# Two layers and two blocks on one core: the inverse root of the row norms partly on GpSimd, the end of the kernel regrouped, retention's gates computed before its projections

## The reference

```python
# stage 0: h = rms_norm(x); stick-breaking attention and a state-space mixer; x = x + mix @ even_w_out
# stage 1: h = rms_norm(x); gated linear attention;                            x = x + mix @ odd_w_out
# stages 2 and 3 (one block each, l = 0 and 1 in the code):
#   h = rmsnorm(x) with scale and shift from c;  proj = h @ w_in
#   attention in three dilated groups, and retention
#   m = sigmoid(g_attn) * (att @ w_proj_attn) + sigmoid(g_ret) * (ret @ w_proj_ret)
#   x = x + gate * (m @ w_out)
# end: out = rmsnorm(x, final_norm_w)
def rms_norm(x, g):
    y = x * rsqrt(mean(x * x, axis=-1) + 1e-6)
    return y * g
```

## Time and profile before

| what | value |
|---|---|
| median of 3 runs | 1077.22 us (1075.8 to 1077.54) |
| the profiled execution | 1076.03 us |
| its span in the profile | 1074.2 us |
| PE busy | 1021.6 us, 95% of the span |
| DVE / ACT / POOL busy | 704.9 / 565.3 / 336.5 us |
| mean granted TensorE clock | 0.987 of full |

### The profile page before, as it was taken

One profiled execution on the slowest core, in us unless ns is written; L12 is line 12 of the kernel. 1 busy time (PEld: TensorE's weight loads), 2 busy tenths in 40 slices (PEclk: granted clock), 3 DMA queues, 4 the chain that ended last, 5 costly groups with the idle time before them and its releaser, 6 DMA issues.

```text
span 1074.2 us, 15495 instructions
## 1 busy us (share of the span) xinstructions
PE 1021.6 (95%) x6084; PEld 900.2 (84%) x6084; DVE 704.9 (66%) x1072; ACT 565.3 (53%) x872; POOL 336.5 (31%) x349
## 2 busy tenths in 40 slices
PE   5999999989999799999999989979999999999995
PEld 5778889878968689998899868868999888998884
DVE  7894856888767664455576686774544565667665
ACT  5978577557344754455443344455444555334552
POOL 4700150433530173552453545321744000320001
PEclk9999999999999999999999989999999999999998
DMA  8543424767736487765565556745877436644531
GB/s 277 154 141 101 141 93 140 251 206 246 216 113 215 145 266 217 241 200 153 177 214 178 164 170 206 225 128 177 249 216 216 122 118 177 185 148 147 187 137 59
DMA packets 94440, 191.12 MB, mean 178 GB/s; under 512 B 6768, under 2 KB 10096, under 8 KB 94368
## 3 DMA queue, kind: packets, MB, share of 16 engines
q1 hardware_dynamic: 86256, 164.71, 49.6%
q0 software_dynamic: 6960, 22.71, 6.8%
q10 hardware_dynamic: 1152, 2.72, 0.7%
HBM read 189.07 MB, written 1.05 MB: 177 GB/s over the span
## 4 chain that ended last, share of the span: by engine, by line
PE 86%; DVE 6%; ACT 5%; DMA 1%; issue 1%; DVEq 0%; SPq 0%; ACTq 0%
PE G L593 15%; PE G L595 14%; PE G L594 14%; PE G L602 8%; PE G L604 8%; PE G L605 8%; PE B L556 2%; DVE WL L1526 1%; ACT AR L1046 1%; ACT WH L1046 1%; PE G L631 1%; PE G L633 1%; PE G L632 1%; DMA RAW<-in_even_w_in 1%; PE B L905 1%
## 5 line engine op out<-in xcount | busy, mean ns | idle before, releaser
L1526 DVE TENSOR_TENSOR WL<-RAW,WH 128x1024 fp32r<-128x1024 f32 (+2 forms) x306 | 398.5, 1306 | 258.2 <-ACT WH L1046 257.4
L1046 ACT ACTIVATE WH<-RAW 128x1024 fp32r<-128x1024 f32 (+2 forms) x306 | 320.2, 1050 | 282.9 <-PE G L595 142.7
L593 PE MATMUL G<-WH,HTh 128*128 128x512 f32 (+1 forms) x564 | 227.7, 404 | 2.8 <-DVE WL L1526 2.5
L602 PE MATMUL G<-HTh,WH 128*128 128x256 f32 x768 | 220.2, 287 | 0.5 <-DVE HTl L1602 0.5
L595 PE MATMUL G<-WL,HTh 128*128 128x512 f32 (+1 forms) x564 | 218.7, 388 | 0.0
L604 PE MATMUL G<-HTl,WH 128*128 128x256 f32 x768 | 217.9, 284 | 0.0
L605 PE MATMUL G<-HTh,WL 128*128 128x256 f32 x768 | 217.8, 284 | 0.0
L594 PE MATMUL G<-WH,HTl 128*128 128x512 f32 (+1 forms) x564 | 217.8, 386 | 0.0
L602 PEld LDWEIGHTS G<-HTh,WH 128*128 128x128 f32 x768 | 147.1, 191 | 2.4 <-issue 2.2
L604 PEld LDWEIGHTS G<-HTl,WH 128*128 128x128 f32 x768 | 147.1, 191 | 0.9 <-issue 0.7
L605 PEld LDWEIGHTS G<-HTh,WL 128*128 128x128 f32 x768 | 147.0, 191 | 0.0
(11 more groups left out here) (344 smaller groups left out, 1343.9 us busy)
## 6 DMA issues: line engine op xcount, KB each, us to landing
RAW<-in_w_in SPq DMA_DIRECT2D x176, 512.0 KB, 3.8
RAW<-in_even_w_in SPq DMA_DIRECT2D x40, 512.0 KB, 3.7
AR<-in_w_ada POOLq DMA_DIRECT2D x80, 256.0 KB, 3.9
RAW<-in_odd_w_in SPq DMA_DIRECT2D x16, 512.0 KB, 4.9
RAW<-in_w_proj_ret SPq DMA_DIRECT2D x16, 512.0 KB, 3.5
RAW<-in_w_out SPq DMA_DIRECT2D x16, 512.0 KB, 4.2
RAW<-in_even_w_out SPq DMA_DIRECT2D x12, 512.0 KB, 3.9
AR<-in_w_ada SPq DMA_DIRECT2D x16, 256.0 KB, 4.3
```

Of the source, the lines that this page charges most:

```text
L593: nc.tensor.matmul(o, xh, wh, start=begins, stop=False)
L602: nc.tensor.matmul(o, fh, h_[:, kx, :], start=begins and f % 2 == 0, stop=False, skip_group_check=True)
L1046: return nc.scalar.activation(out_, ps, ACT.Copy, **kw)
L1526: vt(wl, raw, wh.bitcast(F32), ALU.subtract).then_inc(*dve.mark(LO, n))
```

## The change

- `rstd` is split. POOL's new `root(l, ti)` adds 1024 times epsilon to the sum of the first half, then the sum of the second (`MEAN`), and raises the result to the power -0.5 (`ROOT`). DVE's `rstd` makes -16 times the sum and takes one Newton step on POOL's value, three instructions in place of eleven (ten in norm 0).
- POOL calls `root` before each `scaled`; in stages 3 and norm 4 the root of tile 0 stands ahead of the half-0 add of tile 1 (`RES_P`).
- The end: SP loads `FW` in the middle of block 3's stream. The last residual add is cut in two, and ACT squares the two parts as they come. DVE multiplies (0,0) and (0,1) ahead of the last root, and (1,1) behind it; POOL makes `XW`, the product of (1,0) with `FW`, ahead of its last root, and ACT scales it. SP issues three stores and ACT one.
- In both blocks the groups run `gr0`, `gr1`, `pr0`, `pr1`; `gr1`'s tanh has a tile of its own (`T12b`, the space of `SZA2`), and the first two `mrg_turn`s move from steps 186 and 187 to 194 and 195.

```diff
-AT_MRG = (186, 187, 202, 203)
+AT_MRG = (194, 195, 202, 203)
...
+        NSE = [cols(2) for _ in range(5)]
+        neg_half = cols(1)
...
             for i in range(2):
                 group(("gr", l, i), "N", WI, 10240 + 512 * i, 512, K8, ht, banks())
+            for i in range(2):
                 group(("pr", l, i), "N", t["w_proj_ret_2"][l], 512 * i, 512, K8, lambda k: (YTh, YTl, 4 + k), banks())
...
-                            act.wait_ge(*MRG.of(l, 0, ti))
-                        nc.scalar.activation(T12[:, ti, :], ps[:, :], ACT.Tanh, scale=0.5).then_inc(
+                            act.wait_ge(*ATT_G.of(l))
+                        nc.scalar.activation((T12b if (kind, i) == ("gr", 1) else T12)[:, ti, :], ps[:, :], ACT.Tanh, scale=0.5).then_inc(
                             *act.mark(SIG, kind, l, i, ti))
...
-            for ti in range(2):
-                for n in range(2):
-                    square(3, ti, n)
-            nc.scalar.dma_start(FW, t["final_norm_w_2"].rearrange("(a n) -> a n", a=1).partition_broadcast(P)).then_inc(
-                l_fw, 16)
-            xs = X[:, 0, 512:1024]
-            act.wait_ge(*RSTD.of(4, 0))
-            copy(xs, xs, scale=NR[4][:, 0:1]).then_inc(*act.mark(FIN_A, "x"))
-            act.wait_ge(*FIN_P.of(0, 1))
-            nc.scalar.dma_start(out[0, 0:128, 512:1024], xs).then_inc(s_out[1], 16)
-            act.wait_ge(*FIN.of(1, 1))
-            nc.scalar.dma_start(out[0, 128:256, 512:1024], X[:, 1, 512:1024]).then_inc(s_out[3], 16)
+            square(3, 0, 0)
+            square(3, 0, 1)
+            square(3, 1, 0)
+            for j in range(2):
+                c = slice(512 + 256 * j, 768 + 256 * j)
+                act.wait_ge(*FIN_X.of(j))
+                nc.scalar.activation(TK[:, 1, 1, 256 * j:256 * j + 256], X[:, 1, c], ACT.Square,
+                                     accum_out=ss_last if j else NSS[4][:, 3:4]).then_inc(
+                    *(act.mark(FIN_SQ, "last") if j else act.mark(SUMSQ, 4, 1, 1)))
+            act.wait_ge(*RSTD.of(4, 1))
+            act.wait_ge(*FIN_W.of("x"))
+            copy(X[:, 1, 0:512], XW, scale=NR[4][:, 1:2]).then_inc(*act.mark(FIN_A, "x"))
+            act.wait_ge(*FIN_A.of("x"))
+            nc.scalar.dma_start(out[0, 128:256, 0:512], X[:, 1, 0:512]).then_inc(s_out[2], 16)
...
-                i, h, z, e, v = (x[:, k] for x in (rs_i, rs_h, rs_z, rs_e, rs_v))
-                inv = 1.0 / 1024
-                if l == 0:
-                    dve.wait_ge(*SUMSQ.of(0, ti))
-                    ts(v, NSS[0][:, k], inv, EPS, ALU.mult, ALU.add).then_inc(*dve.tick())
-                else:
-                    dve.wait_ge(*SUMSQ.of(l, ti, 0))
-                    ts(e, NSS[l][:, k], inv, EPS, ALU.mult, ALU.add).then_inc(*dve.tick())
-                    dve.wait_ge(*dve.prev)
-                    dve.wait_ge(*SUMSQ.of(l, ti, 1))
-                    ts(v, NSS[l][:, 2 + ti:3 + ti], inv, e, ALU.mult, ALU.add).then_inc(*dve.tick())
+                h, z = (x[:, k] for x in (rs_h, rs_z))
+                dve.wait_ge(*MEAN.of(l, ti))
+                ts(h, NSE[l][:, k], -16.0, None, ALU.mult).then_inc(*dve.tick())
                 dve.wait_ge(*dve.prev)
-                ts(i.bitcast(I32), v.bitcast(I32), 1, None, ALU.logical_shift_right).then_inc(*dve.tick())
-                first = dve.prev
-                ts(h, v, -0.5, 0.0, ALU.mult, ALU.add).then_inc(*dve.tick())
-                half = dve.prev
-                dve.wait_ge(*first)
-                ts(y.bitcast(I32), i.bitcast(I32), -1.0, MAGIC, ALU.mult, ALU.add).then_inc(*dve.tick())
-                dve.wait_ge(*half)
-                for step in range(3):
-                    dve.wait_ge(*dve.prev)
-                    stt(z, y, h, y, ALU.mult, ALU.mult).then_inc(*dve.tick())
-                    dve.wait_ge(*dve.prev)
-                    stt(y, z, 1.5, y, ALU.add, ALU.mult).then_inc(*(dve.tick() if step < 2 else dve.mark(RSTD, l, ti)))
+                dve.wait_ge(*ROOT.of(l, ti))
+                stt(z, y, h, y, ALU.mult, ALU.mult).then_inc(*dve.tick())
+                dve.wait_ge(*dve.prev)
+                stt(y, z, 48.0, y, ALU.add, ALU.mult).then_inc(*dve.mark(RSTD, l, ti))
...
-                        stt(T12[:, ti, :], T12[:, ti, :], 1.0, ps[:, :], ALU.add, ALU.mult).then_inc(*dve.tick())
+                        s = (T12, T12b)[i][:, ti, :]
+                        stt(s, s, 1.0, ps[:, :], ALU.add, ALU.mult).then_inc(*dve.tick())
                         dve.wait_ge(*dve.prev)
                         dve.wait_ge(*MRG_A.of(l, i, ti))
-                        vt(m, m, T12[:, ti, :], ALU.add).then_inc(*dve.mark(MRG, l, i, ti))
+                        vt(m, m, s, ALU.add).then_inc(*dve.mark(MRG, l, i, ti))
...
+                    if (l, ti) == (1, 1):
+                        for j in range(2):
+                            c = slice(256 * j, 256 * j + 256)
+                            vt(x[:, c], x[:, c], G2[:, 1, c], ALU.add).then_inc(*dve.mark(FIN_X, j))
+                        return
...
-            rstd(4, 1)
-            for ti, n in ((0, 0), (1, 0), (1, 1)):
+            dve.wait_ge(l_fw, 16)
+            for ti, n in ((0, 0), (0, 1), (1, 1)):
                 c = slice(512 * n, 512 * n + 512)
                 xs = X[:, ti, c]
+                if ti:
+                    rstd(4, 1)
                 dve.wait_ge(*RSTD.of(4, ti))
-                dve.wait_ge(l_fw, 16)
-                stt(xs, xs, NR[4][:, ti:ti + 1], FW[:, c], ALU.mult, ALU.mult).then_inc(*dve.mark(FIN, ti, n))
+                stt(xs, xs, NR[4][:, ti:ti + 1], FW[:, c], ALU.mult, ALU.mult).then_inc(*dve.mark(FIN_V, ti, n))
...
+            def root(l, ti):
+                e, y = NSE[l][:, ti:ti + 1], NR[l][:, ti:ti + 1]
+                pool.wait_ge(*SUMSQ.of(l, ti, 0) if l else SUMSQ.of(0, ti))
+                gts(e, NSS[l][:, ti:ti + 1], 1024 * EPS, 0.0, ALU.add, ALU.add).then_inc(
+                    *(pool.tick() if l else pool.mark(MEAN, 0, ti)))
+                own()
+                if l:
+                    pool.wait_ge(*SUMSQ.of(l, ti, 1))
+                    gts(e, NSS[l][:, 2 + ti:3 + ti], e, 0.0, ALU.add, ALU.add).then_inc(
+                        *(pool.tick() if (l, ti) == (4, 1) else pool.mark(MEAN, l, ti)))
+                    own()
+                if (l, ti) == (4, 1):
+                    pool.wait_ge(*FIN_SQ.of("last"))
+                    gts(e, ss_last, e, 0.0, ALU.add, ALU.add).then_inc(*pool.mark(MEAN, l, ti))
+                    own()
+                gtt(y, e, neg_half, ALU.pow).then_inc(*pool.mark(ROOT, l, ti))
...
+            nc.gpsimd.memset(neg_half, -0.5).then_inc(*pool.tick())
             for ti in range(2):
+                root(0, ti)
                 scaled(0, ti)
...
             for ti in range(2):
+                root(1, ti)
                 scaled(1, ti)
...
+                    if ti == 0:
+                        root(2 + l, 0)
+                scaled(2 + l, 0)
+                root(2 + l, 1)
+                scaled(2 + l, 1)
                 for step in range(212):
                     time = 2 * H0[l] + step
...
+                if ti == 0:
+                    root(4, 0)
             pool.wait_ge(l_fw, 16)
-            gtt(x, x, FW[:, 512:1024], ALU.mult).then_inc(*pool.mark(FIN_P, 0, 1))
+            own()
+            gtt(XW, x, FW[:, 0:512], ALU.mult).then_inc(*pool.mark(FIN_W, "x"))
+            root(4, 1)
...
+                if n == H0[1] + 54:
+                    sp.wait_ge(*ADA_P.of(1, 63))
+                    nc.sync.dma_start(FW, t["final_norm_w_2"].rearrange("(a n) -> a n", a=1).partition_broadcast(
+                        P)).then_inc(l_fw, 16)
+            for ti, n in ((0, 0), (0, 1), (1, 1)):
+                sp.wait_ge(*FIN_V.of(ti, n))
+                nc.sync.dma_start(out[0, 128 * ti:128 * ti + 128, 512 * n:512 * n + 512],
+                                  X[:, ti, 512 * n:512 * n + 512]).then_inc(s_out[2 * ti + n], 16)
             for s in s_out:
                 sp.wait_ge(s, 16)
```

More of the change, by code:

```diff
@@ L288, in program @@
         FW = AR[:, 1024:2048]
+        XW = flat(QKT[:, 0:2, :])
+        ss_last = cols(1)
         WE, WEO, WG = t["even_w_in"][0], t["even_w_out"][0], t["s5_w_glu"][0]
@@ L427, in program @@
         SUMSQ = events("sumsq", [(0, 0), (0, 1)] + [(l, ti, n) for l in range(1, 5) for ti in L2 for n in L2])
+        MEAN, ROOT = (events(f"norm_{x}", [(l, ti) for l in range(5) for ti in L2]) for x in ("mean", "root"))
         RSTD = events("rstd", [(l, ti) for l in range(5) for ti in L2])
```

12 lines of the change are left out of this document (3 added, 9 removed).

## The result

The changed kernel takes 1068.79 us, the median of six runs. One of them took 1276.3 us at a mean clock of 0.752 and is left out of the ratio; the other five lie between 1065.52 and 1071.91, and their median is 1068.22. The kernel before, measured beside it, takes 1076.68. The ratio is 0.992 with a 95% interval of 0.9896 to 0.9945, so the gain is about 8 us where 11.6 were forecast. The time lies inside the range and 3.2 us above the predicted 1065.6. Measured again in a later group of runs it came to 1067.65 (ratio 0.9909, 0.9897 to 0.9922).

A forecast was written before the change was run, and what follows sets the result against it. Bound by what keeps TensorE (95% busy) waiting or lies before its first and after its last product. Start +0.7, boundaries -1.9, -2.4, -1.5, clock -2.2, end -4.3, regrouping 0: -11.6 us, median 1065.6, range 1062.0 to 1071.5.

The forecast's parts named there:

- the start: Before TensorE's first product: roots queue behind POOL's memsets, moving that product from 16.40 to 17.1, a cost of 0.7 us.
- the end: After TensorE's last product: early FW load, products ahead of the root and an earlier last store gain 4.3 us.
- What the move is worth between the stages: Boundaries 0/1, 1/2 and 2/3: shorter DVE roots gain 1.9, 2.4 and 1.5 us, the second tile giving the larger gain.
- The power: POOL's power in each root: taken as 0.3 us, with a range of 0.15 to 1.3.
- Boundary 2/3: Between stages 2 and 3: POOL's order eats the first tile's gain, the second tile's mostly stays; 1.5 us gained.
- the moved add is hidden: At the end, POOL's tile 1 add moves 0.6 us behind tile 0's root, its square still done in time.
- The clock: Slow stretches at boundaries 1/2 and 2/3: 1.6 and 2.7 us at full clock; half taken, 2.2 us, bounds 0 and 4.3.
- rival 2: Boundaries 1/2 and 2/3: the clock falls as before, 2.2 us less gain, 1067.8 us; chance 0.14.
- rival 1: Boundaries 1/2 and 2/3: the clock stays up at both, 2.1 us more gain, 1063.5 us; chance 0.17.
- The regrouping: Gate groups in both blocks: the back-to-back merges fit, worth 0, with -0.3 to +1.0 us for both blocks.
- The slope of the power: Each us of power costs 2 at the start, 1 at boundary 2/3, 1 at the end; above 1.0 us, 2 more.
- the balance at 2.3 us: POOL's power length at which gain and loss are equal; beyond it the change is slower, chance 0.07 with rounding.

The follow-up runs named there:

- e11: Changed kernel with norm 0's roots and all roots of tile 0 back on DVE, POOL keeping four roots of tile 1: 1066.75 us, ratio 0.9909.
- e2: Changed kernel with all ten roots back on DVE in their old form, the new end and regrouping kept: 1075.66 us, ratio 0.9986.
- e3: Changed kernel with the two roots of norm 0 back on DVE: 1064.54 us, ratio 0.9875.
- e10: e9 with POOL's add of tile 1 also waiting for tile 0's finished root between stages 2 and 3: 1065.66 us, ratio 0.991.
- e12: The changed kernel once more, unaltered, in a later group of runs: 1067.65 us, ratio 0.9909.
- e8: e3 with the last residual add and its square uncut, so POOL's last root has two sums: 1064.22 us, ratio 0.9885.
- e9: e8 with POOL's add of tile 1 at the end waiting until DVE has finished tile 0's root: 1064.94 us, ratio 0.9889.
- e1: Kernel before with only the regrouped gates, including the second tanh tile and two moved turns: 1077.12 us, ratio 0.9998.
- e6: e3 with each of the eight remaining powers on POOL made twice in a row: 1068.18 us, ratio 0.9923.
- e4: Changed kernel with the roots of norm 0 and norm 4 back on DVE, POOL keeping the six at the boundaries: 1066.44 us, ratio 0.9889.
- e5: e3 with POOL's add of tile 1 again ahead of tile 0's root, at boundary 2/3 and the end: 1066.78 us, ratio 0.9911.
- e7: e3 with unread products filling TensorE's waits at the three boundaries: 1065.83 us, ratio 0.9904.

## Why the prediction was right, and where it was wrong

The sign, the order of size and the main mechanism held. The time came out 3.2 us above the forecast, because two terms of the sum, the start and the end, were too good by 1.0 and 2.75 us, and the clock's 0.8 us behind 1/2 did not come in this run. Behind 2/3 the forecast had 1.5 us and 1.35 for the clock; 3.4 came.

- **What the move is worth between the stages: right.** Second tiles: DVE is freed of 1.6 us (2.22 to 0.63 in the rows of boundary 1/2), POOL has the value long before, and tile 1 carries most of the gain (e11). From the first product to the turn at 2/3, 4.3 us were forecast without the clock, and 4.0 came. In e2, where DVE keeps the roots, the turning of tile 1 is back in its old place.
- **The power: mis-sized.** I took 0.3 us, near the row of a 128x16 product, with 0.15 to 1.3 as bounds. It is 0.56 or 0.57 in all ten of its instances. The bounds held it.
- **The start: mis-sized, +0.7 became +1.66.** The slope of 2 us for each us of power is right: it gives +1.24 for the true power. Of the rest, 0.2 us are small steps and POOL's first scaling (0.98 where I had put 0.8), and 0.2 come behind the roots, with DVE's 0.21 us of wait for `HTh`. Each step of the chain has a hand-over of its own, as the 0.08 us between the sum's end at 10.78 and the power at 10.86, and I had counted only some. "First product near 17.1" was wrong (18.06). e3, which undoes this part alone, has the first product at 16.44.
- **Boundary 2/3: mis-sized, -1.5 became -3.4** (0.36 lost ahead of the first turn, 3.7 gained behind it). That the first tile gains nothing there was right, and so was the reason, ACT's order: ACT goes from its weight piece to the turned tile without a pause at 712.20, but 0.5 us later than I had it, because POOL's root took 1.10 us and not 0.6. POOL's add also holds DVE's Newton half for 1.32 us and puts off the turning; taking that hold away by postponing the add (e10) did not bring the first product forward. The statement that the moved add is hidden failed at the end. Behind the turn I had counted the 1.65 us of the root, and 1.35 for the clock. Both waits of the second tile went, 3.35 together: 1.6 by the root, and the rest because the slow products now fill the time.
- **The clock: neither half nor all, but one or the other.** In the profiled run it fell as before behind all three turns, as rival 2 has it, and at 2/3 only the place of the fall moved. But e12, the same kernel, has 0.89, 0.89 and 1.00, and e3 and e8, the same code up to the end, have 1.00, 1.00, 0.79 and 1.00, 0.89, 1.00: whether it falls differs from one execution to the next. Behind 1/2 a run with 1.00 is 1.1 to 2.0 us shorter (357.36 and 357.86 in e9 and e3 against 358.97 to 359.35 in e8, e12 and the changed kernel, all with 0.83 over the 20 us from 626 to 646, around the fall in block 2), which agrees with the 1.6 worked out from the cold stretch. Behind 2/3 it is 0.3 to 0.6 (344.87 to 345.03 against 345.30 and 345.45), not 2.7, since DVE's chain takes over as soon as TensorE is faster: the waits of 0.46 and 1.32 us are then there (e8). So behind 2/3 rival 1 and rival 2 make nearly the same time, and the sum had put them 2.7 us apart there.
- **The end: mis-sized, -4.3 became -1.55.** This is the term that was furthest off. In five pieces, before and after: last product to last residual 0.40 and 0.77; to the last sum 2.17 and 2.51; to the end of the root 2.11 and 2.34; to the last store's issue 4.10 and 0.79; to the span's end 2.69 and 3.51. The fourth piece, the load of `FW` out of the way and the products made early, gave 3.3 us as forecast. The other four were each too good: by 0.73, 0.18, 1.14 and 0.8 us. I had the last root end 1.2 us after the sum, and it took 2.34, no shorter than DVE's eleven instructions: a sum stretched to 1.02, another of 0.29, a power of 0.57, and the hand-overs. The held Newton half delayed the last residual by 0.73. In the kernel before the last store was issued 0.7 us or more behind the others and the span ended 2.69 us later; now two stores of 256 KB are issued together at 1063.1, and it ends 3.51 us later. It is 3.40 to 3.53 in every run with the new end; that the second store is the cause is not shown. From last product to last issue it was 6.41 us, where I had said 4.4 (8.78 before).
- **The regrouping: right**, 0 (e1). So was that cutting the last add brings at most 0.2 us (e8).
- **The slope of the power: right in the main.** e6 gives some 3 us for each us of power without the start, between the 2 and the 4 that I had. No run had a power slow enough to try the balance at 2.3 us.

What remains open: what decides whether the clock falls in an execution, what the end of the span owes to the paired stores, and what an order would look like in which DVE and POOL do not meet at all in the last 10 us. e4, e5, e9 and e10 moved the meeting and did not remove it.

The kernel e3 (roots of norm 0 left on DVE) at 1064.54 and e8 (with the last add whole besides) at 1064.22 us beat both kernels, the changed one by 3.1 to 4.6 us, depending on which of its two medians is taken. About 1.7 of that is the start.

## What to carry to other kernels

Moving the chain of small instructions to the idle engine paid where the value was wanted late, behind a queue (the second tiles: 8.9 of 11.1 us in e11). It cost 1.66 us at the start, where all wait for the chain itself, and behind the last sum the root took 2.34 us, 2.11 before: count every hand-over there, not only the instructions. Before placing a wide two-input instruction of GpSimd, look at what DVE starts in the same microsecond (here 1.33 us in place of 0.22), and search the trace at hand for a small instruction that is twice as long as its like: it was there in the kernel before (0.47 in place of 0.22). A stretch at the low clock cost here only what TensorE would not have waited anyway: price it by the waits that follow it, not by its length alone. In a dense stretch that was all of it (6.5 of 6.8 us in e7), ahead of a wait for another engine little (0.3 to 0.6 us at boundary 2/3, where 2.7 were forecast).

## What the runs showed of the hardware

- GpSimd's power on one column of 128 rows took 0.55 to 0.58 us in all instances of these runs but two, which took 0.84 beside a wide instruction of DVE (e6). Most of its sums of one column took 0.21 to 0.29 us. Beside DVE's wide instructions they took up to 1.02 in the changed kernel (1059.73) and 1.28 in e6 (353.26).
- A DVE SCALAR_TENSOR_TENSOR of one column that started 0.04 us before GpSimd's 128x512 add of two inputs lasted 1.32 to 1.34 us, to the end of that add, and 0.22 without it (e9). Beside the same add DVE's TENSOR_SCALARs of one column took 0.14 to 0.21 us, as without it (kernel before). A 128x512 product of DVE with `FW` took 1.75 us beside GpSimd's product, and 0.74 otherwise (e9); DVE's product of a bank with the gate took 0.68 beside the same product of GpSimd (1057.45 in the changed kernel).
- Around waits of 1.3 to 2.1 us at the three boundaries the same code had a granted clock of 1.00 in one execution and 0.89 or 0.79 over 16 us in another. In the one profiled execution with the waits filled (e7) it was 1.00 behind all three turns, but 0.69 over 22 us in which TensorE was busy throughout. In or right behind the wait of 4.7 to 4.9 us in block 2 it fell in all fourteen profiled runs.
